# Queries and keys of the chunk and stick-breaking heads made token-major, ones at TensorE's start, the last columns in two banks

## The reference

```python
def first_block(...):                       # pool_layer, nsa_layer
    return rmsnorm(h, final_g)
...
qkv = rmsnorm_2(x, attn_norm) @ w_qkv       # 2048 x 6144
# diff heads: 8, q and k of 2 x 64 columns, v of 128
# stick-breaking heads: 8, q, k, v of 64     -> qb, kb, vb below, 512 columns each
# chunk heads: 8, q, k, v of 64, band of 64s -> qc, kcc, vcc below, 512 columns each
x = x + heads @ w_o
h = rmsnorm_2(x, ffn_norm)
g, u = h @ w_gate, h @ w_up                 # 2048 x 5632 each
x = x + (silu(conv3(g)) * u) @ w_down
return rmsnorm_2(x, final_norm)
```

## Time and profile before

| | |
|---|---|
| three runs | 2006.02, 2006.98, 2007.39 us; median 2006.98 |
| the profiled execution | own time 2005.24 us, span 2003.4 us |
| TensorE busy | 1987.2 us, 99% of the span |
| VectorE, ScalarE, GpSimd busy | 1499.9, 1065.5, 400.8 us |
| read from memory | 370.92 MB |

### The profile page before, as it was taken

How to read it: one execution, slowest core, us unless ns; L and a number is a source line. 1 busy time by engine, 2 the same in 40 slices (tenths; PEclk the granted TensorE clock), 3 DMA queues, 4 the chain that set the end, 5 groups by cost and what they waited for, 6 DMA issues and landing times.

```text
span 2003.4 us, 27138 instructions
## 1 busy us (share of the span) xinstructions
PE 1987.2 (99%) x10380; PEld 1696.5 (85%) x10380; DVE 1499.9 (75%) x2180; ACT 1065.5 (53%) x1619; POOL 400.8 (20%) x379
## 2 busy tenths in 40 slices
PE   8999999999999999999999999999999999999998
PEld 7888988888888888888888888888888888888886
DVE  6776778788798666877656678688899545989954
ACT  6654544467534554654555555455555444555544
POOL 0014544300000444420222235200000100000120
PEclk9999999999999999999999999999999999999999
DMA  9664666567655334556444445655655655555564
GB/s 341 226 192 150 192 187 198 190 210 238 221 172 169 126 116 137 186 204 196 161 159 157 148 157 190 206 184 185 199 189 192 203 191 187 194 195 190 191 206 150
DMA packets 103795, 374.80 MB, mean 187 GB/s; under 512 B 11729, under 2 KB 13169, under 8 KB 103153
## 3 DMA queue, kind: packets, MB, share of 16 engines
q1 hardware_dynamic: 103376, 372.54, 56.8%
q10 hardware_dynamic: 288, 0.52, 0.1%
HBM read 370.92 MB, written 2.10 MB: 186 GB/s over the span
## 4 chain that ended last, share of the span: by engine, by line
PE 98%; DVE 1%; DMA 0%; ACT 0%; issue 0%; SPq 0%; ACTq 0%
PE psg L586 27%; PE psg L587 14%; PE psg L653 7%; PE psg L654 7%; PE psg L655 7%; PE pss L653 4%; PE pss L654 4%; PE pss L655 4%; PE pst L683 2%; PE pss L683 2%; PE pss L685 2%; PE pss L684 2%; PE pst L685 2%; PE pst L684 2%; PE psg L627 1%; PE pst L627 1%
## 5 line engine op out<-in xcount | busy, mean ns | idle before, releaser
L1855 DVE TENSOR_TENSOR s_w<-s_stage,s_w 128x1024 fp32r<-128x1024 f32 (+2 forms) x690 | 855.6, 1242 | 314.7 <-ACT s_w L1214 310.5
L1214 ACT ACTIVATE s_w<-s_stage 128x1024 fp32r<-128x1024 f32 (+2 forms) x690 | 725.5, 1053 | 667.0 <-PE psg L587 313.2
L586 PE MATMUL psg<-s_ry,s_w 128*128 128x512 f32 x1216 | 429.4, 394 | 0.2 <-DVE s_w L1855 0.2
L586 PE MATMUL psg<-s_rh,s_w 128*128 128x512 f32 x1216 | 427.6, 394 | 0.3 <-DVE s_w L1855 0.3
L587 PE MATMUL psg<-s_rh,s_w 128*128 128x256 f32 x1216 | 342.7, 282 | 0.0
L587 PE MATMUL psg<-s_ry,s_w 128*128 128x256 f32 x1216 | 342.6, 282 | 0.0
L586 PEld LDWEIGHTS psg<-s_ry,s_w 128*128 128x128 f32 x1216 | 228.3, 188 | 51.3 <-issue 4.1
L586 PEld LDWEIGHTS psg<-s_rh,s_w 128*128 128x128 f32 x1216 | 228.3, 188 | 48.9 <-issue 1.0
L587 PEld LDWEIGHTS psg<-s_rh,s_w 128*128 128x128 f32 x1216 | 229.8, 189 | 0.6
L587 PEld LDWEIGHTS psg<-s_ry,s_w 128*128 128x128 f32 x1216 | 229.8, 189 | 0.2
L653 PE MATMUL psg<-s_w,s_ry 128*128 128x512 f32 x512 | 201.2, 393 | 0.0
(11 more groups left out here) (424 smaller groups left out, 2973.9 us busy)
## 6 DMA issues: line engine op xcount, KB each, us to landing
s_stage<-in_wo SPq DMA_DIRECT2D x96, 512.0 KB, 3.5
s_stage<-in_wg SPq DMA_DIRECT2D x88, 512.0 KB, 3.3
s_stage<-in_wu SPq DMA_DIRECT2D x88, 512.0 KB, 3.3
s_stage<-in_wd SPq DMA_DIRECT2D x88, 512.0 KB, 3.4
s_stage<-in_ain SPq DMA_DIRECT2D x64, 512.0 KB, 3.7
s_stage<-in_wkv SPq DMA_DIRECT2D x32, 512.0 KB, 3.4
s_stage<-in_bq SPq DMA_DIRECT2D x24, 512.0 KB, 3.4
s_stage<-in_bzq SPq DMA_DIRECT2D x24, 512.0 KB, 3.2
```

Of the source, the lines that this page charges most:

```text
L586: e.matmul(o, M.WH[:, r, ws], xx, start=begin, stop=False)
L1214: e.activation(M.weights(c, 0, n, shift), M.staged(c, n), ACT.Copy).then_inc(S["wh"], 1)
L1855: e.tensor_tensor(M.weights(c, 1, n, shift), M.staged(c, n), M.weights(c, 0, n, shift), ALU.subtract).then_inc(S["wl"], 1)
```

## The change

Three places change, and the small loads' semaphores are merged.

1. `qc`, `kcc`, `qb` and `kb` (32 units) take the pair form, with their weight columns packed like those of the gate and up blocks (`t_pack`). `block`, `evacuate` and `turns` become common to both. ScalarE takes both banks out into a new buffer `EV2` with 1/rms (times 0.125 for the queries, `RCS`), VectorE turns them, and `ch_pair` and `sb_pair` wait for the turned result; the two calls for `qc` that the diff shows below stand for those of all four. The 16 multiplies of `eff_norms` come 14 ticks later.
2. TensorE begins with 11 products of ones (128 columns each, fp32) into a bank that nothing reads then. In unit 0 the four products with the high weights come ahead of the four with the low ones for each k (`first_unit`). Unit 1 too comes, and is split, in halves, ahead of blocks 2 and 3 of the memory; the memory's piece of four blocks becomes two of two; ScalarE, VectorE and SyncE get their first work in the new order.
3. At the end `last_columns` does t = 1 of the last three units in two passes of 256 columns, the second into another bank; the sums of the first three column blocks and their scaled form are made ahead, the squares of the last block in two halves, GpSimd makes two of the multiplies, and the stores are four of 128 x 1024.

```diff
-MEMP = ((0, 1), (1, 2), (2, 4), (4, 8), (8, 12), (12, 16))
+MEMP = ((0, 1), (1, 2), (2, 4), (4, 6), (6, 8), (8, 12), (12, 16))
...
-    P.group([("qc", j) for j in range(4)], "qc")
-    for j in range(4):
-        P.tile(("kcc", j), P.halves("kc", j))
+    P.block("qc", "qc")
+    P.block("kcc", "kc")
     P.pair("vcc", "vc")
-    for n in ("qb", "kb"):
-        for j in range(4):
-            P.tile((n, j), P.halves(n, j))
+    P.block("qb", "qb")
+    P.block("kb", "kb")
...
+    def first_unit(tiles, x, ready):
+        for t in tiles:
+            held[P.bank[t]] = P.out[t]
+        for k in range(2):
+            xh, xx, _ = x(k)
+            ready(k)
+            w.wait_ge(("wh_a", "wh")[k], 1)
+            for n in range(4):
+                ws = slice(512 * k + 128 * n, 512 * k + 128 * n + 128)
+                e.matmul(M.product(P.bank[tiles[n]])[:, :], M.WH[:, 0, ws], xx, start=k == 0, stop=False)
+            w.wait_ge(("wl_a", "wl")[k], 1)
+            for n in range(4):
+                ws = slice(512 * k + 128 * n, 512 * k + 128 * n + 128)
+                m = e.matmul(M.product(P.bank[tiles[n]])[:, T:2 * T], M.WL[:, 0, ws], xh, start=False, stop=False)
+        m.then_inc(S["units"], 1)
...
+        def last_columns(c):
+            for h in range(2):
+                if h:
+                    vacant(("s", 0))
+                o = last_bank(M) if h else down_bank(M, 3, 1)[:, 0:256]
+                for u in range(nk // 2 - 3, nk // 2):
+                    r = (c + u - nk // 2 + 3) % NR
+                    for kk in range(2):
+                        k = 2 * u + kk
+                        xh, _, xl = x(k)
+                        ws = slice(SHIFT + 512 * kk + 256 * h, SHIFT + 512 * kk + 256 * h + 256)
+                        e.matmul(o, xh[:, 128:256], M.WH[:, r, ws], start=h == 1 and k == nk - 6, stop=False)
+                        e.matmul(o, xh[:, 128:256], M.WL[:, r, ws], start=False, stop=False)
+                        m = e.matmul(o, xl[:, 128:256], M.WH[:, r, ws], start=False, stop=k == nk - 1)
+                    if h:
+                        m.then_inc(S["units"], 1)
+                        unit()
+                if not h:
+                    m.then_inc(S["down"], 1)
...
+    w.wait_ge("eps", 1)
+    for n in range(11):
+        e.matmul(M.PSO[0][:, 0:128], ones, ones, start=True, stop=True)
     side.start(token_rows("mem_c", 15))
...
+    evacuate("qc", M.EV2, M.RCS, "eff_c")
...
+    side.start(turns("qc", M.QC, M.EV2))
...
         w.wait_ge("sqc2", KT)
+        for _ in range(14):
+            yield
         for j in range(KT):
             w.wait_ge("hcl", j + 1)
             e.scalar_tensor_tensor(M.X[:, j, :], M.X[:, j, :], M.vec("fing", j), M.RB[0][:, :], ALU.mult, ALU.mult).then_inc(S["x2"], 1)
...
+    def finish():
+        add_last(0)
+        refine_last(0)
+        scale_last(0, 1536, 2048)
+        fourth_sum()
+        add_last(1)
+        refine_last(1)
+        x = M.OT[:, 1, 0:512]
+        e.tensor_scalar(x, x, M.FR[:, 1:2], None, ALU.mult).then_inc(S["f_dve"], 1)
+        scale_last(1, 1792, 2048)
+        w.wait_ge("xg", 7)
+        x = M.OT[:, 1, 1536:1792]
+        e.tensor_scalar(x, x, M.FR[:, 1:2], None, ALU.mult).then_inc(S["f_dve"], 1)
...
+    w.wait_ge("f_dve", 9)
+    w.wait_ge("xg", 1)
+    x = M.OT[:, 0, block(0)]
+    e.tensor_scalar(x, x, M.FR[:, 0:1], None, ALU.mult).then_inc(S["f_pool"], 1)
+    w.wait_ge("sqx", 8)
+    x = M.OT[:, 1, 1536:1792]
+    e.tensor_tensor(x, x, M.FG[:, 1536:1792], ALU.mult).then_inc(S["xg"], 1)
...
-    for n in range(3):
-        memory(n)
+    memory(0)
+    memory(1)
+    for half, name in enumerate(("st_b", "st1")):
+        ws = slice(512 * half, 512 * half + 512)
+        e.dma_start(M.ST[:, 1, ws], P.units[1][0][:, ws]).then_inc(S[name], 16)
+        issued[0] = 2
+    memory(2)
     weights()
     memory(3)
     weights()
     memory(4)
+    memory(5)
     weights()
-    memory(5)
+    memory(6)
+    weights()
     e.dma_start(M.V[:, 16:NVEC], A["vec"][:, 16:NVEC]).then_inc(S["l_vec"], 16)
-    weight_units(4)
+    weight_units(2)
...
+    store(0, 1024, 2048)
...
+    store(0, 0, 1024)
...
+    store(1, 0, 1024)
...
+    store(1, 1024, 2048)
```

More of the change, by code:

```diff
@@ L184, in __init__ @@
         self.takes = 0
+        self.turned = {}
         self.counts = {"out": 0, "out_act": 0}
@@ L245, in residual, with block @@
             self.tile((name, j), units(j))
-    def block(self, m):
-        tile = ("ff", m)
+    def block(self, tile, name, b=0, banks=None):
+        self.turned[tile] = len(self.turned) * 4
         for t in range(2):
-            self.bank[tile, t] = ("sg"[m % 2], t)
+            if banks:
+                self.bank[tile, t] = (banks, t)
+            else:
+                self.take((tile, t))
         for u in range(8):
-            self.unit(self.A[("wg", "wu")[m % 2]][8 * (m // 2) + u], 1024, SHIFT)
+            self.unit(self.A[name][8 * b + u], 1024, SHIFT)
             if u == 7:
@@ L702, in down @@
                 products(n, u, (c + u - apart) % NR, [(0, 0), (1, 0)])
-            for u in range(apart, nk // 2):
-                products(n, u, (c + u - apart) % NR, [(0, 1), (1, 1)]).then_inc(S["units"], 1)
-                unit()
+            if apart < nk // 2:
+                last_columns(c)
     def flips():
@@ L1165, in eff_hook @@
         side.start(eff_norms())
-    group([("qc", j) for j in range(4)], Y, ready("hc"), eff_hook)
-    for j in range(4):
-        tile(("kcc", j), Y, ready("hc"))
+    pair("qc", Y, ready("hc"), eff_hook)
+    pair("kcc", Y, ready("hc"))
     pair("vcc", Y, ready("hc"))
@@ L1172, in tensor_program @@
         side.start(later(6 * p, ch_pair(p)))
-    for n in ("qb", "kb"):
-        for j in range(4):
-            tile((n, j), Y, ready("hc"))
+    pair("qb", Y, ready("hc"))
+    pair("kb", Y, ready("hc"))
     pair("vb", Y, ready("hc"))
@@ L1250, in v_pair, with evacuate @@
         nxt()
+    def evacuate(tile, ev, rc, n):
+        w.wait_ge("nr_dve", 3 * NORM[n] + 3)
+        if P.turned[tile]:
+            w.wait_ge("turned", P.turned[tile])
+        for t in range(2):
+            if t:
+                w.wait_ge("units", P.end[tile, 1])
+            else:
+                w.wait_ge("half", P.half[tile])
+            src = M.product(P.bank[tile, t]).rearrange("p (r f) -> p r f", r=4)
+            e.activation(ev[:, :, t, :], src, ACT.Copy, scale=rc[:, t:t + 1]).then_inc(S["out_act"], 1)
     def put_y(y, R, j):
@@ L2395, in gate_block @@
             w.wait_ge("ff_v", 2 * (2 * m))
-        for q in range(4):
-            turn(m, q, M.GG)
-            yield
+        yield from turns(("ff", m), M.GG, M.EV)
         for c in range(4):
@@ L2410, in up_block @@
             w.wait_ge("ff_h", 2 * m - 2)
-        for q in range(4):
-            turn(m, q, M.UU)
-            yield
-        w.wait_ge("turned", 4 * m + 4)
+        yield from turns(("ff", m), M.UU, M.EV)
+        w.wait_ge("turned", P.turned["ff", m] + 4)
         for c in range(4):
@@ L2538, in vector_program @@
     side.start(eff_norms())
-    nxt(3)
+    nxt(5)
     normed("eff")
-    for j in range(4):
-        scaled(("qc", j), M.QC[:, j, :], 0.125, 1)
-        if j % 2:
-            nxt()
-    tiles("kcc", 4, M.KCC, None, 1)
+    side.start(turns("qc", M.QC, M.EV2))
+    nxt(8)
+    side.start(turns("kcc", M.KCC, M.EV2))
     v_pair("vcc", M.VCC[:, 0, :], 1, "eff_c")
```

257 lines of the change are left out of this document (156 added, 101 removed).

## The result

The changed kernel takes 2009.50 us (median of 22 runs, 2007.53 to 2011.55), the kernel before, on the same chips, 2006.26 (22 runs): 3.2 us slower, ratio 1.0016 with an interval of 1.0011 to 1.0022. The forecast was 2004.2, so 2.0 faster than this median of before. The profiled execution took 2010.74 with a span of 2008.9.

A forecast was written before the change was run, and what follows sets the result against it. TensorE, busy 99% of the span, bounds the kernel. Start -1.0, middle -1.73 and 0, end 0 sum to -2.75 us: 2002.5 from the profiled 2005.24, 2004.2 from the median 2006.98; own range 2003.0 to 2005.4, whole range 2001.6 to 2006.5.

The forecast's parts named there:

- The form: Middle: 32 units go from tile to pair form, 2.772 to 2.718 us each on TensorE, 1.73 us less.
- Rival B: Middle: only the columns count, so the new form saves nothing there; sum -1.0, 2006.0 us; chance 0.10.
- the price by the issue gap: Middle: a Trainium skill rule, N/2.4 + 2.5 ns a product, by which the 32 units save only 0.3 us.
- What the other engines do instead: Middle: VectorE's transposes and moved multiplies and ScalarE's copies cost TensorE nothing: 0, with +8.2 us as upper bound.
- the lead of VectorE's low parts over TensorE: Middle, four groups: some 2.2 us of lead stand against 1.1 us that VectorE runs late by a group's end.
- The start: First units: unit 1 begins at 9.9 rather than 11.16, unit 2 at 12.95; -1.0 us, bounds -2.5 and -0.3.
- the ones' share: Start: 11 products of ones raise the clock for unit 0; if they leave it low, -0.3 us instead of -1.0.
- The end: Behind the last products: two passes, sums made ahead, fewer stores, GpSimd's multiplies; 0 taken, bounds -0.8 and +1.3 us.
- GpSimd's two operations: End: GpSimd's multiplies, 1.72 and 0.86 us, run in the same microseconds as VectorE's scalings; +0.6 us put on that.
- Rival D: End: VectorE waits out GpSimd's two multiplies in full; end +2.6, sum -0.15, 2006.8 us; chance 0.08.
- C: Middle: VectorE reaches the transposes without lead and TensorE waits; about 8.2 us, net +5.5, 2012.5 us; chance 0.06.
- A: Start: gives its whole wait back, -2.5 us; with the middle's -1.73 the sum is -4.2, 2002.8 us; chance 0.22.

The follow-up runs named there:

- m1: Kernel before with the first part of the change alone (pair form, turns, multiplies 14 ticks later), start and end as before: 2010.86 us against 2005.57.
- m6: Kernel before with the second part of the change alone (ones, unit 1 in halves, new order of loads): 2004.25 us against 2005.90.
- m8: Kernel before with the second part of the change alone, without the 11 products of ones: 2003.98 us against 2005.90.
- m7: Kernel before with the third part of the change alone (last columns in two passes, other sums and stores): 2005.63 us against 2005.90.
- m3: Changed kernel with the 16 multiplies 60 ticks later instead of 14, behind the chunk heads: 2005.10 us against 2005.57 of the kernel before.
- m9: Kernel before with only the 16 multiplies moved 14 ticks later; tiles, start and end as before: 2006.91 us against 2005.77.
- m2: Kernel before with the second and third part of the change, without the first: 2003.77 us against 2005.57.
- m10: Changed kernel with the 16 multiplies in their old place, without the delay: 2006.51 us against 2005.77 of the kernel before.

## Why the prediction was wrong

**The form: right.** 0.054 us a unit was forecast, and the units in which TensorE does nothing else show it (2.72 instead of 2.77). Where other products stand between (units 304 to 306, 330, 331 and others) the difference is 0.03 or less, and units 300, 310 and 324, at or near a change from one form to another, differ by more (0.15, 0.11 and 0.17). With the steps of the waits taken off, units 300 to 351 are 1.6 us shorter, against the sum of 1.73. Rival B falls with it, and with it the price by the issue gap that the prediction set beside the rows.

**What the other engines do instead: the step that failed.** "I take 0" rested on one resource, the lead of VectorE's low parts over TensorE. That reading was correct as far as it went: in the changed kernel TensorE waits for no low part at the four groups. But a tick holds more than its split. The chunk heads' chain passes through the same ticks of VectorE and ScalarE, twice through VectorE, and ends at a place on TensorE that is fixed in units; the timeline of before had its margin in two rows, GpSimd done at 990.83 and TensorE there at 991.55. The prediction asked whether TensorE's next unit would be ready and did not ask what else is queued behind a tick of 3.0 us. Its sentence that the heads' own products stretch the units and so cover the multiplies had the sign wrong: those products are what was held up. It also misread the multiplies: it put four of them into each of four ticks, 1.9 us a tick, but `eff_norms` makes one a tick, and in the changed kernel they stand from 929.54 to 979.51, the first twelve ahead of the turns of `qb` and beside the chunk heads' first two pairs. In size this term was 0 and measured +7.8 in the profiled execution, 1.65 of it the clock's, and in the runs 5.3 + 1.6 (m1, with the form's gain taken off) = 6.9. How the chain's delay divides between the turns, the copies and GpSimd's longer scalings (4.79 for 3.71) is not shown.

**The start: right.** -1.0 was forecast with bounds of -0.3 and -2.5; the second part alone gives -1.7. The data's landing, not the clock, set unit 1's start in the changed kernel, as said. The prediction put the ones' share at 0.7, the step from its bound of -0.3, with the clock left low, to -1.0. In the profiles they gain 0.9 by unit 3 (m6 against m8), but the medians of m6 and m8 are 0.3 apart the other way: over the whole kernel the ones paid nothing that can be measured.

**The end: right.** 0 was forecast, m7 gives -0.3, the profile of the changed kernel -0.8; m6 keeps the old end, and in its profile too the stretch behind the last product is 0.6 shorter, so the -0.8 means little. GpSimd's two operations, which the prediction priced at +0.6, did not hold VectorE's last scalings (0.49 and 0.48 each), because they were done by 2003.25 and the scalings begin at 2003.86. One sum of a single column beside the first of them took 0.58 where its neighbours take 0.15; that GpSimd held it is likely and not tested. Rival D falls.

**The rivals.** C had the sign and the engine: VectorE late around the turns, worst where the multiplies meet them, priced at 8.2 against 7.8. That the two lie so near is luck: 3.8 of the 8.2 were for multiplies four to a tick, and 1.65 of the 7.8 is the clock's. It had the wrong wait: for low parts instead of GpSimd's scaled weights, and its condition, a lead of 2.2 us used up, was not the one that decided; a margin of 0.7 was. It got 0.06, though the two rows of the margin stood in the trace of before. A did not come: the start's data were as late as reckoned.

That the copies on ScalarE delay the exponentials of the second pair is read from the timeline alone (they wait there for TensorE's half units ahead of L1580); no run takes them away without the turns, so their share against the turns' is argued and not shown.

## What to carry to other kernels

When work is added to an in-order engine that has idle time on average, list every chain that passes through the ticks in question and read for each when its result is ready and when the consumer comes; the smallest of these margins decides, not the engine's load. Margins and idle time are shared: two edits that each cost nothing at a place (unit 341 in m3 and m9) can cost 2 us there together, so measure them together and apart. Where a consumer's place is written as a count of units, moving it by one unit is the cheap cure, but every step behind it on the other engines moves with it and needs its own margin.

## What the runs showed of the hardware

A wait of TensorE of 2.07 us (changed kernel) was followed by 3.7 us at a granted clock of 0.54, one of 1.97 (m2) by 3.3 us at 0.50, and one of 2.03 at the same place as the first (m1) by none (1.00 throughout). So the length of the wait alone did not decide; the first fall cost 1.65 us more. GpSimd's four scalings of one pair of chunk heads took between 3.61 and 5.75 us (second and last pair of m10), and between 3.71 and 4.79 in the kernel before; what VectorE did beside them differs, and no run shows which of its operations counts.
